# Scan stage: kernel rows of two pairs side by side in TensorE's column halves, weight transposes in two groups; attention: four probability buffers

## The chip, the core and the metric

The kernel runs on one NeuronCore of a Trainium2 chip. The metric is device time of one execution in microseconds (us). Engines are named as in the profile: PE is TensorE (PEld its weight loads), DVE is VectorE, ACT is ScalarE, POOL is GpSimd, SP is the engine that issues the DMAs here. All data is float32; the profile shows a float32 matmul as two records, one behind the other, and a transpose as one.

## The reference, cut to what matters

The reference is a first block (an S5 state-space mixer and an HGRN2 mixer, then a gated feed-forward part) and a second block of two layers, the second of which has attention with 8 heads. Two places matter here.

The S5 mixer has 64 groups of 16 channels with 64 complex states each, over 1040 tokens (padded to 1056):

```python
v_re = jnp.einsum('blgh,gph->blgp', uf, bb_re)
v_im = jnp.einsum('blgh,gph->blgp', uf, bb_im)
_, _, s_re, s_im = lax.associative_scan(_complex_affine_combine, (a_re, a_im, v_re, v_im), axis=1)
y = (jnp.einsum('blgp,ghp->blgh', s_re, c_re)
     - jnp.einsum('blgp,ghp->blgh', s_im, c_im)
     + d_skip.reshape(SSM_GROUPS, SSM_GROUP) * uf)
```

The attention of the second block takes 1024 queries against 1280 keys in 8 heads:

```python
s = jnp.einsum('bqhd,bkhd->bhqk', qi, k) * scale
p = jax.nn.softmax(s, axis=-1)
return jnp.einsum('bhqk,bkhd->bqhd', p, v)
```

## The kernel before, in words

The program is a chain of phases with a barrier of all engines between them. The change touches two: the scan (function `s5`, 937 to 1063 us of the span) and the attention (function `attend`, 2816 to 3202 us). Every engine has an instruction stream written out by hand and runs it in order; semaphores tie them together.

**Scan.** Tokens are cut in chunks of 8 (`TAU`), so that 132 chunks stand side by side (`NCH`). Two groups make a pair, whose 2 x 64 states fill the 128 partitions. There are 32 pairs, in 4 rounds (`n`) of 8; each round is worked in three trips of 3, 3 and 2 pairs, so there are 12 trips `f = 3n + trip`. The parts of the work:

- `turn(n)` on PE transposes a round's 16 input-weight tiles (4 fills of a PSUM bank with 4 transposes each); `turn_out(n)` on ACT copies each fill to `win`.
- `kernel(n)` on PE makes the kernel rows (how an input of a chunk acts on later outputs of the same chunk) of 8 pairs: for each pair four matmuls with a 128x64 weight (two parts, each with 128 and 112 columns, lines 1107 and 1108) and one with a 64x64 weight and 32 columns for the skip term (line 1110). It fills two PSUM banks, four pairs each, and uses 64 of their 128 partitions. `kernel_out(n)` on ACT copies each bank, in 8 activations, to the shifted places of `toep`.
- `inputs(f)` on PE (line 1138) brings a trip's inputs to the states, with outputs alternating between PSUM partitions 0 to 63 and 64 to 127. `turned_back(f)` and `states_of(f)` on DVE make the states of all chunks.
- `outputs(f)` on PE sums, in `psy`, `toep` times the inputs (line 1153) and the state part (line 1161). `gelus(f)` on ACT empties it (line 1223), and SP stores the result.

The order on PE for a trip f is: for trip 0, `turn(n+1)`; `inputs(f+2)`; for trip 1, `kernel(n+1)`; `outputs(f)`. On ACT it is: for trip 0, `turn_out(n+1)`; for trip 1, `kernel_out(n+1)`; `gelus(f)`; for trip 2, `spread_b(n+2)` and `decays(n+2)`. `turn` and `kernel` share the two banks of `pk`: fill number e, 6 in a round, goes to bank e % 2 and first waits for fill e - 2 to be copied out (`pk_used`). `outputs(f)` waits for `gelus(f-1)` and for the states of f. `inputs(3n)` waits for the four transposed fills of its round. SP loads the next weights to transpose (`load_wt(n+2)`) once the last of the round's four fills is made.

**Attention.** 32 steps s, four to a head (j = s % 4), two blocks of 128 queries in a step. On PE a step is: scores of the two blocks (line 2559); the 20 transposes of the probabilities of the step before in five PSUM fills (line 2589), with the sums over values between them (line 2606); and, for j = 0, 1, 2, pieces of the next head's queries and keys. ACT copies two of the five fills, then makes the two exponentials of the step (line 2695); DVE takes the row maxima (line 2781), copies three fills (line 2728), and takes the reciprocals of the sums (line 2797) once both exponentials are done; POOL then scales both blocks (line 2823), for which the next step's transposes wait. The probabilities of block i = 2s + ab are in `pr[i % 3]`: the exponential of block i waits until the transposes of block i - 3 are all made, for the second block of a step those of the same step on PE.

## Time and profile before

| | us |
|---|---|
| median of 3 runs | 3392.8 (3386.49 to 3393.48) |
| the profiled execution | 3391.3 |
| its span, first to last instruction | 3389.5 |
| around the span | 1.8 |
| scan stage, 937 to 1063 | 126 |
| attention stage, 2816 to 3202 | 386 |

Over the whole span PE is busy 3138.0 us (93%), DVE 1991.5 us, ACT 940.7 us and POOL 151.0 us. A timeline row gives start, duration, engine, line, operation, what is written and read, the shapes and a count; in square brackets stands how long the engine was idle before it and what ended that. A row with a count covers so many records from its start on. Where one row of the same engine begins before the end of the one before, the distance of the starts is the rate at which the work goes.

### The profile page before, as it was taken

The numbers are of one execution on the slowest core, as the hardware profiler recorded it, in microseconds if no ns is written. First come the engines' busy times: TensorE is split into PE (matmuls) and PEld (weight loads), VectorE is DVE, ScalarE is ACT, GpSimd is POOL, SyncE is SP. The second block draws the span as 40 slices with busy tenths as digits, with TensorE's granted clock in tenths as the row PEclk, the third lists the DMA queues.
The fourth block names the chain that finished last, engine by engine and source line by source line (L and its number), as shares of the span: only waits on it lengthen the run. The fifth ranks groups of instructions, "written<-read, shape, count | busy, mean of one in ns | idle before, by whom it ended". The sixth has DMA issues, their size and how long they took to land. (4 is left out here: it accounts for less than half of the span.)

```text
span 3389.5 us, 47701 instructions
## 1 busy us (share of the span) xinstructions
PE 3138.0 (93%) x20182; PEld 2905.0 (86%) x20182; DVE 1991.5 (59%) x2836; ACT 940.7 (28%) x1315; POOL 151.0 (4%) x124
## 2 busy tenths in 40 slices
PE   7999999998887999999999999999898977888787
PEld 7999999998876999999999998999898964555565
DVE  6666777664766455663574466444545526776446
ACT  5221222222444211211111112121323323444323
POOL 0000000000000000000000000000031001222200
PEclk9999999999988999999999999999898988999898
DMA  4223333333374344113213214111121330000121
GB/s 146 87 95 96 94 102 98 108 107 136 119 119 126 110 137 143 51 47 122 75 44 100 94 44 149 51 40 46 56 69 60 135 124 0 1 1 1 73 96 69
DMA packets 101822, 285.74 MB, mean 84 GB/s; under 512 B 13540, under 2 KB 32484, under 8 KB 100328
## 3 DMA queue, kind: packets, MB, share of 16 engines
q1 hardware_dynamic: 101608, 282.69, 26.1%
q8 instruction: 159, 2.61, 0.3%
q14 instruction: 55, 0.45, 0.0%
HBM read 218.79 MB, written 63.85 MB: 83 GB/s over the span
## 5 line engine op out<-in xcount | busy, mean ns | idle before, releaser
L471 PE MATMUL mixer_in_dense<-mix_z_high,mixer_in_whigh 128*128 128x348 f32 x1312 | 431.6, 329 | 15.3 <-DVE mixer_in_wlow L565 10.4
L471 PE MATMUL mixer_in_dense<-mix_z_high,mixer_in_wlow 128*128 128x348 f32 x1312 | 427.2, 326 | 0.0
L471 PE MATMUL mixer_in_dense<-mix_z_low,mixer_in_whigh 128*128 128x348 f32 x1312 | 426.4, 325 | 0.0
L1449 PE MATMUL flow_dense<-rst_norms_operand_b_high,flow_whigh 128*128 128x342 f32 x1248 | 399.5, 320 | 0.4 <-DVE flow_wlow L1542 0.4
L1449 PE MATMUL flow_dense<-irst_norms_operand_b_low,flow_whigh 128*128 128x342 f32 x1248 | 398.6, 319 | 0.0
L1449 PE MATMUL flow_dense<-rst_norms_operand_b_high,flow_wlow 128*128 128x342 f32 x1248 | 397.7, 319 | 0.0
L2012 PE MATMUL joint_dense<-rst_norms_operand_b_high,joint_whigh 128*128 128x342 f32 (+2 forms) x1056 | 344.6, 326 | 18.3 <-DVEq L2129 10.5
L2012 PE MATMUL joint_dense<-rst_norms_operand_b_high,joint_wlow 128*128 128x342 f32 (+2 forms) x1056 | 341.4, 323 | 0.0
L2012 PE MATMUL joint_dense<-irst_norms_operand_b_low,joint_whigh 128*128 128x342 f32 (+2 forms) x1056 | 340.4, 322 | 0.0
L1449 PE MATMUL flow_dense<-first_operand_a_high,flow_whigh 128*128 128x342 f32 (+1 forms) x912 | 291.6, 320 | 17.3 <-DVEq L1563 17.3
L1449 PE MATMUL flow_dense<-first_operand_a_low,flow_whigh 128*128 128x342 f32 (+1 forms) x912 | 292.1, 320 | 0.0
L1449 PE MATMUL flow_dense<-first_operand_a_high,flow_wlow 128*128 128x342 f32 (+1 forms) x912 | 291.4, 320 | 0.0
L471 PEld LDWEIGHTS mixer_in_dense<-mix_z_high,mixer_in_whigh 128*128 128x128 f32 x1312 | 251.6, 192 | 19.6 <-issue 16.9
L471 PEld LDWEIGHTS mixer_in_dense<-mix_z_low,mixer_in_whigh 128*128 128x128 f32 x1312 | 251.1, 191 | 0.0
L471 PEld LDWEIGHTS mixer_in_dense<-mix_z_high,mixer_in_wlow 128*128 128x128 f32 x1312 | 251.0, 191 | 0.0
L1492 ACT ACTIVATE flow_whigh<-first_norms_weights 128x1024 fp32r<-128x1024 f32 (+1 forms) x92 | 95.6, 1039 | 559.9 <-PE flow_dense L1449 536.9
L1449 PEld LDWEIGHTS flow_dense<-rst_norms_operand_b_high,flow_whigh 128*128 128x128 f32 x1248 | 235.3, 189 | 1.3 <-issue 1.2
L1449 PEld LDWEIGHTS flow_dense<-rst_norms_operand_b_high,flow_wlow 128*128 128x128 f32 x1248 | 235.2, 188 | 0.1
L1449 PEld LDWEIGHTS flow_dense<-irst_norms_operand_b_low,flow_whigh 128*128 128x128 f32 x1248 | 234.6, 188 | 0.0
L2012 PEld LDWEIGHTS joint_dense<-rst_norms_operand_b_high,joint_whigh 128*128 128x128 f32 x1056 | 202.0, 191 | 23.9 <-DVEq L2129 8.4
L2012 PEld LDWEIGHTS joint_dense<-rst_norms_operand_b_high,joint_wlow 128*128 128x128 f32 x1056 | 202.6, 192 | 0.6 <-issue 0.5
L2012 PEld LDWEIGHTS joint_dense<-irst_norms_operand_b_low,joint_whigh 128*128 128x128 f32 x1056 | 203.0, 192 | 0.0
(549 smaller groups left out, 5872.3 us busy)
## 6 DMA issues: line engine op xcount, KB each, us to landing
mixer_in_wstage<-w_in SPq DMA_DIRECT2D x56, 512.0 KB, 4.9
mixer_in_mod_w<-w_mod SPq DMA_DIRECT2D x64, 384.0 KB, 3.6
first_norms_weights<-w_up SPq DMA_DIRECT2D x44, 512.0 KB, 3.4
flow_side<-h SPq DMA_DIRECT2D x24, 512.0 KB, 5.1
h<-flow_out SPq DMA_DIRECT2D x24, 512.0 KB, 3.5
first_norms_weights<-ab_w_in SPq DMA_DIRECT2D x20, 512.0 KB, 3.5
p<-mixer_in_out SPq DMA_DIRECT2D x16, 528.0 KB, 2.8
first_norms_weights<-w_down SPq DMA_DIRECT2D x16, 512.0 KB, 3.8
```

The source lines that it names most:

```text
L471: mm = pe.matmul(bank(s)[:, 0:W], a[n % 2][:, P * m:P * (m + 1)], z[x][:, m, W * b:W * (b + 1)], start=m == 0 and i == 0, stop=m == DT - 1 ...
L1449: mm = pe.matmul(o, w[n % NW][:, P * k:P * (k + 1)], x[h][:, k, where], start=k == 0 and e == 0, stop=k == kt - 1 and e == 2)
L1492: act.activation(wh[n % NW][:, 0:w], stage[n % 2][:, 0:w], ACT.Copy).then_inc(high_ready, 1)
L2012: mm = pe.matmul(pd[s % 2][:, 0:wide], a[n % 2][:, P * k:P * (k + 1)], m, start=k == 0 and e == 0, stop=k == DT - 1 and e == 2)
```

## The change

In the scan, `kernel(n)` takes pairs two at a time: the first pair's output goes to PSUM partitions 0 to 63 and the second's to 64 to 127, with the same instructions alternating between them, so that all eight pairs fill one bank. The fills of a round are 5 instead of 6, and the one kernel fill is announced once. `kernel_out(n)` waits once and copies both halves: 16 activations, as before, now of every second pair. `turn` is called in two halves, two fills ahead of `inputs(f+2)` and two behind it. In the attention, the probabilities have four buffers instead of three, so the exponential of block i waits for the transposes of block i - 4.

```diff
--- before.py
+++ after.py
@@ -1036,7 +1036,7 @@
     urow = t["u_chunks"].rearrange("m p x -> (m p) x").rearrange("(g h) (t c) -> t h g c", h=SG, t=TAU)
     yrow = t["y_chunks"].rearrange("m p x -> (m p) x").rearrange("(g h) (t c) -> t h g c", h=SG, t=TAU)
     trips = ((0, 3), (3, 6), (6, 8))
-    NT3, TURNS, FILLS, WIDE = len(trips), 4, 6, 3
+    NT3, TURNS, FILLS, WIDE = len(trips), 4, 5, 3
     LAST = NT3 * ROUNDS
     with Phase(nc, "scan") as ph:
         U = ph.sb("u", (P, G, NCH))
@@ -1095,32 +1095,34 @@
 
                 def kernel(n):
                     pe.wait_ge(spread, n + 1)
-                    for i in range(2):
-                        o4 = bank(FILLS * n + TURNS + i)
+                    o8 = bank(FILLS * n + TURNS)
+                    for u in range(4):
+                        o = [o8[SS * side:SS * side + SS, P * u:P * u + P] for side in range(2)]
+                        first = u == 0
+                        for part in range(2):
+                            w = [bb[n % 2][part][:, 2 * u + side, :] for side in range(2)]
+                            v = [ca[:, NQ * n + 2 * u + side, part, :, :].rearrange("p k h -> p (k h)") for side in range(2)]
+                            for side in range(2):
+                                pe.matmul(o[side], w[side][:, SG:5 * SG], v[side][:, 0:P], start=first and part == 0,
+                                          stop=False, skip_group_check=True)
+                            for side in range(2):
+                                pe.matmul(o[side][:, SG:P], w[side][:, 0:4 * SG], v[side][:, 0:P - SG], start=False,
+                                          stop=False, skip_group_check=True)
+                        for side in range(2):
+                            mm = pe.matmul(o[side][:, 0:2 * SG], c["ident"][0:SS, 0:SS], skip_diag[:, NQ * n + 2 * u + side, :],
+                                           start=False, stop=True, skip_group_check=True)
+                    mm.then_inc(pk_full, 1)
+
+                def turn(n, part):
+                    if part == 0:
+                        pe.wait_ge(wt_in, 16 * (n + 1))
+                    for half in range(2):
+                        o = bank(FILLS * n + 2 * part + half)
                         for u in range(4):
-                            pair = 4 * i + u
-                            pp = NQ * n + pair
-                            o = o4[0:SS, P * u:P * u + P]
-                            for part in range(2):
-                                w = bb[n % 2][part][:, pair, :]
-                                v = ca[:, pp, part, :, :].rearrange("p k h -> p (k h)")
-                                pe.matmul(o, w[:, SG:5 * SG], v[:, 0:P], start=part == 0, stop=False, skip_group_check=True)
-                                pe.matmul(o[:, SG:P], w[:, 0:4 * SG], v[:, 0:P - SG], start=False, stop=False,
-                                          skip_group_check=True)
-                            mm = pe.matmul(o[:, 0:2 * SG], c["ident"][0:SS, 0:SS], skip_diag[:, pp, :], start=False,
-                                           stop=True, skip_group_check=True)
+                            mm = pe.transpose(o[:, P * u:P * u + P],
+                                              wt[:, part, 4 * half + u, :, :].rearrange("p k h -> p (k h)"),
+                                              c["ident"][:, :])
                         mm.then_inc(pk_full, 1)
-
-                def turn(n):
-                    pe.wait_ge(wt_in, 16 * (n + 1))
-                    for part in range(2):
-                        for half in range(2):
-                            o = bank(FILLS * n + 2 * part + half)
-                            for u in range(4):
-                                mm = pe.transpose(o[:, P * u:P * u + P],
-                                                  wt[:, part, 4 * half + u, :, :].rearrange("p k h -> p (k h)"),
-                                                  c["ident"][:, :])
-                            mm.then_inc(pk_full, 1)
 
                 def inputs(f):
                     n, trip = divmod(f, NT3)
@@ -1163,16 +1165,19 @@
                                 if part == 1 and pair == hi_ - 1:
                                     mm.then_inc(y_full, 1)
 
-                turn(0)
+                turn(0, 0)
+                turn(0, 1)
                 inputs(0)
                 inputs(1)
                 kernel(0)
                 for f in range(LAST):
                     n, trip = divmod(f, NT3)
                     if trip == 0 and n + 1 < ROUNDS:
-                        turn(n + 1)
+                        turn(n + 1, 0)
                     if f + 2 < LAST:
                         inputs(f + 2)
+                    if trip == 0 and n + 1 < ROUNDS:
+                        turn(n + 1, 1)
                     if trip == 1 and n + 1 < ROUNDS:
                         kernel(n + 1)
                     outputs(f)
@@ -1193,15 +1198,16 @@
                         [P, NQ, NCH - 1]), ACT.Copy).then_inc(decayed, 1)
 
                 def kernel_out(n):
-                    for i in range(2):
-                        e = FILLS * n + TURNS + i
-                        act.wait_ge(pk_full, e + 1)
+                    e = FILLS * n + TURNS
+                    act.wait_ge(pk_full, e + 1)
+                    for side in range(2):
                         for par in range(2):
-                            src = pk[32 * par:32 * par + 32, e % 2, :].rearrange("p (a b) -> p a b", b=P)
+                            r0 = SS * side + 32 * par
+                            src = pk[r0:r0 + 32, e % 2, :].rearrange("p (a b) -> p a b", b=P)
                             for j in range(4):
-                                ins = act.activation(toep[n % 2][32 * j:32 * j + 32, par, 4 * i:4 * i + 4, 32 * j:P],
+                                ins = act.activation(toep[n % 2][32 * j:32 * j + 32, par, side::2, 32 * j:P],
                                                      src[:, :, 0:P - 32 * j], ACT.Copy)
-                        ins.then_inc(pk_used, 1)
+                    ins.then_inc(pk_used, 1)
 
                 def turn_out(n):
                     if n >= 2:
@@ -2487,7 +2493,7 @@
         qh, ql = ([ph.sb(f"{n}{j}", (P, SEQ), F32R) for j in range(2)] for n in ("query_high", "query_low"))
         kh, kl = ([ph.sb(f"{n}{j}", (P, T2), F32R) for j in range(2)] for n in ("key_high", "key_low"))
         r1, r2 = ph.sb("turned_cos", (P, HALF)), ph.sb("turned_sin", (P, HALF))
-        pr = [ph.sb(f"probs{j}", (P, T2)) for j in range(3)]
+        pr = [ph.sb(f"probs{j}", (P, T2)) for j in range(4)]
         PT = [ph.sb(f"turned_probs{j}", (P, NKT, HALF)) for j in range(2)]
         yp, ytmp = ph.sb("attended", (P, SEQ)), ph.sb("odd_keys", (P, HALF))
         dg = ph.sb("gate", (P, 4, SEQ))
@@ -2587,7 +2593,7 @@
                                 pe.wait_ge(normal, 2 * s + ab + 1)
                             c0 = P * k if ab == 0 else (CTX + P * k if k < 8 else P * (k - 8))
                             mm = pe.transpose(o[:, 256 * kk + P * ab:256 * kk + P * ab + P],
-                                              pr[(2 * s + ab) % 3][:, c0:c0 + P], c["ident"][:, :])
+                                              pr[(2 * s + ab) % 4][:, c0:c0 + P], c["ident"][:, :])
                     mm.then_inc(full, 1)
 
                 def value_sums(H, pairs):
@@ -2690,9 +2696,9 @@
                         for ab in range(2):
                             i = 2 * s + ab
                             act.wait_ge(biased, s + 1)
-                            if i >= 3:
-                                act.wait_ge(full, ring[("t", (i - 3) // 2, 4)] + 1)
-                            act.activation(pr[i % 3][:, :], pS[:, T2 * ab:T2 * (ab + 1)], ACT.Exp, scale=scale,
+                            if i >= 4:
+                                act.wait_ge(full, ring[("t", (i - 4) // 2, 4)] + 1)
+                            act.activation(pr[i % 4][:, :], pS[:, T2 * ab:T2 * (ab + 1)], ACT.Exp, scale=scale,
                                            bias=nb[:, i:i + 1], accum_out=sm[:, i:i + 1]).then_inc(exped, 1)
                     for n in made_at(s):
                         high(n)
@@ -2820,7 +2826,7 @@
                         for ab in range(2):
                             i = 2 * s + ab
                             pool.wait_ge(inverted, s + 1)
-                            pool.tensor_scalar(pr[i % 3][:, :], pr[i % 3][:, :], ri[:, i:i + 1], 1.0, ALU.mult,
+                            pool.tensor_scalar(pr[i % 4][:, :], pr[i % 4][:, :], ri[:, i:i + 1], 1.0, ALU.mult,
                                                ALU.mult).then_inc(normal, 1)
                     H, pairs = sums_at(s)
                     if 4 in pairs and (H // 2) % 2:
```

## Rows read from the trace of the kernel before

**Rows 1.** Busy time by stage: the scan stage and the attention stage

```profile
core 0: us, PE busy (x) PEld busy (x) DVE busy (x) ACT busy (x) POOL busy (x), PEclk, DMA share, GB/s
937.00:1063.00 126.00, 107.14 (x1024) 93.42 (x1024) 89.97 (x168) 54.87 (x123) 2.16 (x2) 0.88 0.59 91
...
2816.00:3202.00 386.00, 341.18 (x1654) 201.64 (x1654) 251.28 (x346) 169.19 (x271) 95.37 (x72) 0.98 0.00 1
```

**Rows 2.** Timeline of PE inside the kernel-row matmuls of scan round 1

```profile
974.22 0.38 PE L1107 MATMUL scan_turned_and_kernel<-ssm_ca,scan_b_re 128*64 128x128 f32 x2
...
974.85 0.35 PE L1108 MATMUL scan_turned_and_kernel<-ssm_ca,scan_b_im 128*64 128x112 f32 x2
...
975.13 0.30 PE L1110 MATMUL scan_turned_and_kernel<-ssm_skip_diag,all_ident 64*64 64x32 f32 x2
...
975.36 0.43 PE L1107 MATMUL scan_turned_and_kernel<-ssm_ca,scan_b_re 128*64 128x128 f32 x2
```

**Rows 3.** Timeline of PE, matmuls whose outputs alternate between the column halves

```profile
972.82 1.57 PE L1138 MATMUL scan_v<-scan_u,scan_win 128*64 128x132 f32 x24
...
2966.68 1.08 PE L2606 MATMUL attn_values_sum<-attn_turned_probs,attn_values 128*64 128x512 f32 x4
...
2967.69 0.66 PE L2589 MATMUL attn_turned<-all_ident,attn_probs 128*128 128x128 f32 x4
```

**Rows 4.** Timeline of ACT in scan round 1: Toeplitz copies and the gelu behind

```profile
979.04 3.49 ACT L1202 ACTIVATE scan_toeplitz<-scan_turned_and_kernel 32x512 f32<-32x512 f32 x8 [5.23 <-PE scan_turned_and_kernel L1110]
...
983.81 3.49 ACT L1202 ACTIVATE scan_toeplitz<-scan_turned_and_kernel 32x512 f32<-32x512 f32 x8 [1.28 <-PE scan_turned_and_kernel L1110]
...
987.33 0.89 ACT L1223 ACTIVATE scan_yv<-scan_y 128x396 f32<-128x396 f32 x2
```

**Rows 5.** Timeline of PE in the scan, where its stages begin

```profile
963.63 1.12 PE L1120 MATMUL scan_turned_and_kernel<-all_ident,scan_wt 128*128 128x128 f32 x4 [2.99 <-ACT scan_toeplitz L1202]
...
988.30 1.17 PE L1153 MATMUL scan_y<-scan_u,scan_toeplitz 128*128 128x132 f32 x8
...
994.05 1.90 PE L1120 MATMUL scan_turned_and_kernel<-all_ident,scan_wt 128*128 128x128 f32 x8 [2.46 <-ACT scan_win L1213]
...
1002.24 0.38 PE L1107 MATMUL scan_turned_and_kernel<-ssm_ca,scan_b_re 128*64 128x128 f32 x2
...
1016.33 1.17 PE L1153 MATMUL scan_y<-scan_u,scan_toeplitz 128*128 128x132 f32 x8
...
1031.61 0.38 PE L1107 MATMUL scan_turned_and_kernel<-ssm_ca,scan_b_re 128*64 128x128 f32 x2
...
1045.69 1.17 PE L1153 MATMUL scan_y<-scan_u,scan_toeplitz 128*128 128x132 f32 x8
...
1061.05 0.50 PE L1161 MATMUL scan_y<-scan_sr,ssm_ca 64*128 64x132 f32 x4 [2.53 <-DVEq L1293]
```

**Rows 6.** Granted clock of two stretches of the scan (columns as Rows 1)

```profile
994.30:997.70 3.40, 3.40 (x24) 2.87 (x22) 2.60 (x5) 1.39 (x3) 0.00 (x0) 0.52 0.49 91
...
1021.60:1028.50 6.90, 6.36 (x36) 5.69 (x36) 5.50 (x13) 2.17 (x5) 0.00 (x0) 0.51 0.16 31
```

**Rows 7.** Waits in the attention stage: waiter, releaser, us in total, times, longest

```profile
ACT attn_probs L2695 <- PE attn_turned L2589: 22.3, 14, 1.7
```

**Rows 8.** Timeline of ACT in attention: second exponentials that waited

```profile
3003.47 1.33 ACT L2695 ACTIVATE attn_probs<-attn_scores,attn_negated_max 128x1280 f32<-128x1280 f32 x1 [1.41 <-PE attn_turned L2589]
...
3012.59 1.33 ACT L2695 ACTIVATE attn_probs<-attn_scores,attn_negated_max 128x1280 f32<-128x1280 f32 x1 [1.74 <-PE attn_turned L2589]
```

**Rows 9.** Timeline of DVE and PE behind that exponential, and DVE at the end

```profile
3003.41 0.69 DVE L2728 COPY attn_turned_probs<-attn_turned 128x512 f32<-128x512 f32 x1 [0.74 <-PE attn_turned L2589]
...
3004.92 0.17 DVE L2797 RECIPROCAL attn_inverse_sum<-attn_sum 128x2 f32<-128x2 f32 x1 [0.82 <-ACT attn_probs L2695]
...
3181.34 0.17 DVE L2797 RECIPROCAL attn_inverse_sum<-attn_sum 128x2 f32<-128x2 f32 x1 [0.82 <-ACT attn_probs L2695]
...
3007.88 0.98 PE L2589 MATMUL attn_turned<-all_ident,attn_probs 128*128 128x128 f32 x7 [0.47 <-POOL attn_probs L2823]
```

## The prediction

> **What bounds the kernel now.** I read the busy time by stage first, then each engine's timeline in the two stages that change, looking only for what ends a wait of PE. In the scan, PE is busy 107.14 of 126 us and DVE 89.97; in the attention PE is busy 341.18 of 386 us and DVE 251.28 [rows 1]. So PE sets the pace in both, with gaps in which it waits for the engine that empties its banks. None of the waits of PE in rows 5 ends with a DMA. Both stages end in a barrier and what follows starts after it, so a microsecond taken off their end comes off the total.
>
> **Scan, the kernel rows.** One pair now takes 1.14 us for the first (974.22 to 975.36), 1.19 for those behind it, eight pairs 9.5 us [rows 2]. Three of its four large matmuls take 0.63 us (974.22 to 974.85), 0.21 each. The fourth starts at 974.85, and the small one only 0.28 later, at 975.13, where 0.19 would do for its 112 columns; the next pair starts 0.23 after that, for 32 columns. Around the small one the form of the weights changes (128x64, 64x64, 128x64). So the four large ones cost 2 x 0.21 + 2 x 0.19 = 0.80 us, and the small one with both changes of form the other 0.39.
>
> With the halves alternating, the nearest row is `inputs`: 24 records, which are 12 matmuls of 132 columns, take 1.40 us (972.82 to 974.22), 0.233 for two side by side [rows 3, 2]. One alone of that width would take 0.21 x 132/128 = 0.22, so two cost little more than one. In the attention two of 512 columns take 1.01 us (2966.68 to 2967.69) [rows 3]; one alone, scaled up from 0.21, would take 0.85, a factor of 1.18. Two pairs then cost 4 x 0.233 = 0.93 by the first, or 0.80 x 1.18 = 0.94 by the second, plus 0.39 and some 0.05 for the second small one: 1.37 us, and four such couples 5.5 us instead of 9.5. The changes of form are halved in number too. If columns and not the rate of records set the time it is 5.3; if the changes of form cost as much per pair as now it is 7.1. I take 5.5, because both rows show the same alternation.
>
> Here the Trainium skill speaks against the change. "TensorE: Matmul & The Clock Gate", Part 3, The mechanism, says that a weight load overlaps running matmuls only where the row group differs, and the two halves share their rows. By that rule they would follow one another and the kernel rows stay at 9.5 us. The 0.233 us for two disagrees with it; what it would give is the first rival.
>
> **Scan, what follows the kernel rows.** The saved 4.0 us don't reach the end, because of the copies. ACT's 8 copies of a bank take 3.49 us, and the first eight now run beside the second half of PE's kernel rows; behind the last record only 3.49 us remain, and then the gelu, 0.89 us [rows 4]. After the change all 16 wait for one announcement: 6.98 us behind the last record. Queued behind them on ACT is `gelus(3n+1)`, for which PE's `outputs(3n+2)` waits, and SP's stores. From the start of the kernel rows to `outputs(3n+2)` it is now 14.1 us in each of three rounds (1002.24 to 1016.33, 1031.61 to 1045.69, and 974.22 to 988.30) [rows 2, 5]. Then: 5.5 + 0.15 to wake ACT + 6.98 + 0.92 + 0.10 = 13.65. Gain 0.43 a round, 1.3 in all. PE fills 4.5 us of ACT's time with `outputs(3n+1)` and `inputs(3n+4)` and then stands 3.6 us idle, where it has no gap now.
>
> **Scan, transposes in two groups.** From `outputs(3n+2)` to the next kernel rows it takes 13.94 us (988.30 to 1002.24) and 15.28 us (1016.33 to 1031.61) [rows 5]. PE makes two fills, then waits 2.46 us for ACT, which must first do a gelu, the spreading and the decay; then come two fills and `inputs(3n+5)`. In the new order `inputs(3n+5)`, 1.05 us for 16 records at the rate above, lies in that wait: gain 1.05 a round, 2.1 for the two. Also moved is what waits for it: the second group sits behind the inputs on PE, and SP's next load of weights waits for its last fill, but that load is needed a round later, so it costs nothing.
>
> **Scan, first round.** PE's wait of 2.99 us at 963.63 [rows 5] is for the second bank of Toeplitz copies. Now kernel(0) ends at 956.0 instead of 960.0, the 16 copies at 963.15 instead of 963.6, and the second fill waits for all of them: an idle stretch of 6.6 us. But then `inputs(2)` need nothing more. By the same durations kernel(1) starts 0.5 us earlier.
>
> **Scan, the end.** The last state part waits 2.53 us for DVE (1061.05) [rows 5]. DVE's last two chains start once `inputs(10)` are through, and these stand behind the kernel rows of round 3, which end earlier by 0.5 + 2 x (0.43 + 1.05) + 4.0 = 7.5 us; `outputs(8)`, from which PE runs to the end, starts only 0.5 + 3 x 0.43 + 2.1 = 3.9 us earlier. DVE gains 3.6 us on PE, more than the wait, which goes; ACT's gelus between the outputs are next. Gain 2.6 us. Sum for the scan: 1.3 + 2.1 + 0.5 + 2.6 = 6.5 us.
>
> **The clock.** After PE's two gaps of 2.5 us the granted clock is about half, the 1.2 GHz level (0.52 and 0.51), for 3.4 and 6.9 us [rows 6]. With all of it at full clock the 13.94 and 15.28 would be 12.4, so it costs 1.5 and 2.9 us. I leave this cost as it is. The new gaps are longer (3.6 us) and the old one shorter (1.4): the clock could recover those 4.4 us, or be low once more in each round, 1.5 us x 3.
>
> **Attention.** The second exponential of a step now never waits for the transposes of its own step. It did 14 times, 22.3 us [rows 7], of two kinds [rows 8]. Behind j = 3 of a head (3003.47, wait 1.41) the exponential runs 1.4 us earlier, but DVE's copy of the fifth fill ends at 4.10, so the reciprocal moves only from 3004.92 to about 3004.15, and POOL with it; the transposes at 3007.88, which waited for POOL, come 0.78 us earlier [rows 9]. This happens behind four of the seven heads that have another behind them, once more in the last head, and at the end, where the reciprocal at 3181.34 also trails a copy by that much [rows 9]: 6 x 0.78 = 4.7 us. The other kind (3012.59, wait 1.74 [rows 8]) gains nothing, for behind it PE has the sums over values, the next head's queries and the scores to do, and no wait for POOL follows. Behind the other three heads no wait for transposes stands at all. What is late next is DVE with its copies, still in the queue ahead of the reciprocal. Bounds: 0 if DVE is late at each place, 6 if the stall ahead of the scores goes too.
>
> **The sum.** 3391.3 - 6.5 - 4.7 = 3380.1 for the profiled execution, which lies 1.5 us below the median of the runs shown; I predict 3380.
>
> **Rivals.** First, the halves follow one another (the page's rule, as a mechanism of this kernel). Kernel rows stay 9.5 us and the copies come behind all of them: 9.5 + 8.15 = 17.65 instead of 14.1 in three rounds and 3.5 us in the first, so each microsecond of kernel rows costs four. The scan is 4 x 4.0 - 6.5 = 9.5 us longer, the total 3391.3 + 9.5 - 4.7 = 3396: slower. It decides from 8.3 us of kernel rows on. For it: one serial announcement is certain. Against: rows 3. Chance 0.08.
>
> Second, the time is swallowed by copies and clock: the new gap of 3.6 us brings a low clock in every round. Scan 6.5 - 4.5 = 2 us, total 3384.6. The skill's "TensorEngine Tiling (Array Packing)", PSUM Bottleneck, has the general form of this: tiling speeds up TensorE but not the emptying of PSUM. Rows 4 agree, with 6.98 us of copies against 5.5 of matmuls. Chance 0.18.
>
> Third, the opposite: no low clock in rounds 2 and 3: 3380.1 - 4.4 = 3375.7. Chance 0.12. Fourth, the fourth buffer does nothing, because DVE takes the place of the wait: 3384.8. Chance 0.10. My forecast, 3377 to 3384, has 0.52.
>
> **How the numbers follow.** The range takes in all but the first rival, the bounds of both sums and the 7 us by which the runs shown differ: 3372 to 3390. Some 0.2% (3386.0 to 3399.6) is what a measurement of this kernel can tell from no change. Faster: the forecast and the third case, and two thirds of the second and fourth, less what scatter takes: 0.72. Same 0.24, with half of the first rival. Slower 0.04.
>
> **What would show it.** Eight pairs of kernel rows in 5.5 us and eight matmul starts alternating; one block of 16 Toeplitz copies of 7 us behind each; a PE wait of 3 to 4 us for a gelu ahead of `outputs(2)`, (5), (8), and none of 2.5 us for DVE at the end; scan stage 119.5 us. In the attention no second exponential waiting for transposes, and the waits for POOL at 3007.88 and its like gone. It is wrong if kernel rows take over 7 us, or if the waits for POOL stay.

## The result, and the profile after

The changed kernel takes 3369.7 us, the median of four runs (3367.9 to 3376.9), against 3390.0 us (3386.5 to 3393.5) before: a ratio of 0.9944, with a 95% interval of 0.9925 to 0.9964. It is faster, by 20 us; I had forecast 11 below the profiled execution. The time lies under the low end of my range, 3372. The profiled execution took 3367.9 us (span 3366.1), 23.4 us less than the 3391.3 of the profiled one of before.

The busy times by stage of the changed kernel answer to [rows 1] (same columns). The third line is the time ahead of the scan's first `inputs`, which the change doesn't touch:

```profile
932.00:1047.00 115.00, 87.02 (x1024) 76.89 (x1024) 89.91 (x168) 55.02 (x125) 2.44 (x2) 0.88 0.64 98
2804.50:3179.00 374.50, 335.27 (x1654) 199.12 (x1654) 248.39 (x344) 166.92 (x270) 95.28 (x72) 0.99 0.00 1
0.00:941.10 941.10, 878.79 (x6342) 857.11 (x6343) 625.73 (x1000) 287.53 (x445) 11.36 (x24) 0.97 0.34 110
```

PE is busy for 20 us less in the scan than in [rows 1], with the same 1024 matmul records; DVE's 90 us are unchanged, and DVE is now the busier of the two. Its waits in the scan, in us, times and longest:

```profile
DVE scan_t L1271 <- PE scan_v L1140: 20.4, 7, 17.2
```

But for the first of 17.2 us, ahead of its first chain, it waits 3.2 us in all; before it was 17.1 (34.3 us in 7 waits, the first again of 17.2).

From the marks of both traces the 23.4 us divide like this (rounding leaves 0.1):

| stretch | before | after | gain |
|---|---|---|---|
| start to first `inputs` of the scan | 945.9 | 941.1 | 4.8 |
| scan, first `inputs` to last gelu | 117.1 | 105.7 | 11.4 |
| last gelu to first matmul of the flow | 16.5 | 17.9 | -1.4 |
| flow and what follows, up to the attention's first matmul (into `attn_scores`, against `all_ones`) | 1701.7 | 1704.8 | -3.1 |
| that matmul to first transposes of probabilities | 56.8 | 53.1 | 3.7 |
| those transposes to the last sum over values | 360.0 | 352.7 | 7.3 |
| the rest | 191.5 | 190.7 | 0.8 |

The second and the sixth line belong to the change, and so does the third, against it. SP issues the eight stores of each trip one behind another, and with the new kernel PE and ACT end the last trips faster than SP gets through them. The rows are the last stores of the scan, before and then after; in `before` the last eight start as the last gelu ends, in `after` 24 follow one another:

```profile
1063.00 3.63 SPq L1085 DMA_DIRECT2D y_chunks<-scan_yv  x8
...
1039.56 12.36 SPq L1085 DMA_DIRECT2D y_chunks<-scan_yv  x24
```

The last store is issued 3.65 us behind the last gelu before and 5.10 behind it after, and from there to the first matmul of the flow it is 12.9 and 12.8 us. So 1.4 us of what PE gained at the end of the scan stay behind with SP.

The first line is the clock: from the start to the scan's first `inputs` PE's clock stood at its 1.2 GHz level for 75 us before and for 63 us after. Over all the profiles below, with identical code up to there, that time goes from 62 to 83 us and the scan's first `inputs` start between 941.1 and 951.2; the change has no part in it. The fifth line is of the same kind: it is 53 to 54 us, with 20 to 22 us of it at the low level, or 56.7 to 57.5 us, with 28 to 30, in kernels with and without the change (56.8 in `split_alone`, 52.8 in `attn_alone`). The fourth isn't the change's either: `attn_alone`, with the old scan, took 1705.0 us there, and all the other profiles took 1702.8 to 1706.5. Why that of before was shorter, with only 3 us less at the low level, is not shown.

PE's timeline in round 1 of the scan, changed kernel, inside the kernel rows (one couple of pairs, and where the next begins), and then where the stages begin; these answer to [rows 2] and [rows 5]:

```profile
970.36 0.44 PE L1106 MATMUL scan_turned_and_kernel<-ssm_ca,scan_b_re 128*64 128x128 f32 x4
970.63 0.36 PE L1109 MATMUL scan_turned_and_kernel<-ssm_ca,scan_b_re 128*64 128x112 f32 x4
970.82 0.39 PE L1106 MATMUL scan_turned_and_kernel<-ssm_ca,scan_b_im 128*64 128x128 f32 x4
971.04 0.36 PE L1109 MATMUL scan_turned_and_kernel<-ssm_ca,scan_b_im 128*64 128x112 f32 x4
971.33 0.30 PE L1112 MATMUL scan_turned_and_kernel<-ssm_skip_diag,all_ident 64*64 64x32 f32 x4
971.57 0.44 PE L1106 MATMUL scan_turned_and_kernel<-ssm_ca,scan_b_re 128*64 128x128 f32 x4
```

```profile
958.62 1.11 PE L1122 MATMUL scan_turned_and_kernel<-all_ident,scan_wt 128*128 128x128 f32 x4 [6.60 <-ACT scan_toeplitz L1208]
...
968.00 0.39 PE L1106 MATMUL scan_turned_and_kernel<-ssm_ca,scan_b_re 128*64 128x128 f32 x4
...
972.77 1.62 PE L1155 MATMUL scan_y<-scan_u,scan_toeplitz 128*128 128x132 f32 x12
...
980.87 2.13 PE L1155 MATMUL scan_y<-scan_u,scan_toeplitz 128*128 128x132 f32 x8 [3.43 <-ACT scan_yv L1229]
...
988.23 1.14 PE L1122 MATMUL scan_turned_and_kernel<-all_ident,scan_wt 128*128 128x128 f32 x8 [1.41 <-ACT scan_win L1219]
...
993.61 0.39 PE L1106 MATMUL scan_turned_and_kernel<-ssm_ca,scan_b_re 128*64 128x128 f32 x4
...
1006.49 1.17 PE L1155 MATMUL scan_y<-scan_u,scan_toeplitz 128*128 128x132 f32 x8 [3.43 <-ACT scan_yv L1229]
```

Four records (two matmuls, one in each half) start within the 0.19 to 0.27 us that two needed. A couple takes 1.21 us (970.36 to 971.57) and eight pairs 4.77 (968.00 to 972.77), where they took 9.5. Then ACT does 7 us of copies, and PE waits 3.43 us for the gelu behind them:

```profile
972.89 7.02 ACT L1208 ACTIVATE scan_toeplitz<-scan_turned_and_kernel 32x512 f32<-32x512 f32 x16 [5.30 <-PE scan_turned_and_kernel L1112]
979.93 0.89 ACT L1229 ACTIVATE scan_yv<-scan_y 128x396 f32<-128x396 f32 x2
```

In the attention the same place as in [rows 8] and [rows 9], in another head (ACT, DVE, PE), and the one place where PE still waits long for POOL, behind the last head:

```profile
2892.02 1.33 ACT L2701 ACTIVATE attn_probs<-attn_scores,attn_negated_max 128x1280 f32<-128x1280 f32 x1 [0.22 <-DVE attn_negated_max L2789]
2893.34 1.32 ACT L2701 ACTIVATE attn_probs<-attn_scores,attn_negated_max 128x1280 f32<-128x1280 f32 x1
...
2894.78 0.69 DVE L2734 COPY attn_turned_probs<-attn_turned 128x512 f32<-128x512 f32 x1 [0.74 <-PE attn_turned L2595]
2895.39 0.15 DVE L2803 RECIPROCAL attn_inverse_sum<-attn_sum 128x2 f32<-128x2 f32 x1
...
2898.07 1.24 PE L2595 MATMUL attn_turned<-all_ident,attn_probs 128*128 128x128 f32 x8
...
3161.25 0.30 PE L2595 MATMUL attn_turned<-all_ident,attn_probs 128*128 128x128 f32 x1 [2.37 <-POOL attn_probs L2829]
```

The second exponential follows the first without a wait. The reciprocal starts 0.61 us behind the start of the copy instead of 1.51 [rows 9], and the transposes at 2898.07 wait for nothing, where those at 3007.88 waited for POOL.

### The profile page after: what moved, and what is told of

It is laid out like the page before. It is cut to its first block and busy times, and to the rows that moved or that the text cites. A ratio compares the mean times of both kernels' runs of the same rounds, so it can differ in the third digit from the quotient of the medians.

```text
span 3366.1 us, 47700 instructions
## 1 busy us (share of the span) xinstructions
PE 3107.0 (92%) x20182; PEld 2881.8 (86%) x20182; DVE 1988.9 (59%) x2836; ACT 938.6 (28%) x1315; POOL 151.0 (4%) x124
## 5 line engine op out<-in xcount | busy, mean ns | idle before, releaser
L471 PE MATMUL mixer_in_dense<-mix_z_high,mixer_in_whigh 128*128 128x348 f32 x1312 | 430.4, 328 | 15.1 <-DVE mixer_in_wlow L565 10.2
```

The lines of the kernel that those rows point to most:

```text
L471: mm = pe.matmul(bank(s)[:, 0:W], a[n % 2][:, P * m:P * (m + 1)], z[x][:, m, W * b:W * (b + 1)], start=m == 0 and i == 0, stop=m == DT - 1 ...
```

## Experiments

My theory from the two traces was: the halves overlap and the copies swallow most of that; the rest of the scan's gain is the split of the transposes, the earlier end, and the clock; the fourth buffer gives 6 to 7 us. The rivals: all of the scan's gain is the halves, or all of it is the luck of the clock. All ratios are against the kernel before, beside the same runs of it, with 95% intervals. "Stage" is the scan from its first `inputs` to its last gelu in the profile: 117.1 us before, 105.7 after.

**The parts.** `scan_alone` is the changed kernel with the three old probability buffers; `attn_alone` is the kernel before with only this edit:

```diff
-        pr = [ph.sb(f"probs{j}", (P, T2)) for j in range(3)]
+        pr = [ph.sb(f"probs{j}", (P, T2)) for j in range(4)]
...
-                            if i >= 3:
-                                act.wait_ge(full, ring[("t", (i - 3) // 2, 4)] + 1)
+                            if i >= 4:
+                                act.wait_ge(full, ring[("t", (i - 4) // 2, 4)] + 1)
```

`after_again` is the changed kernel as it is.

> The changed kernel with three probability buffers again: the scan edits alone. Theory (parts add, what is left over is the clock's phase): from the first input matmul to the last gelu the scan takes 105 to 108 us instead of 117.1, the attention stays as it was, the total is 9 to 11 us below the kernel before. Rival (the fourth buffer carries most): 4 us or less below.

> The kernel before with four probability buffers: the buffer alone. Theory: one microsecond at each of the four even heads, some 0.2 at the odd ones, and about 2 in the last head: 6 to 7 us below the kernel before. By the predicted reckoning (0.78 at six places): 4.7. Rival (the 10 us that the attention stage lost in the profiled run are all the buffer's): 10.

> The changed kernel once more. Theory: 16 to 19 us below the kernel before, and the stages ahead of the scan last as long as how often the clock is low in them says, not 5 us less than before each time. Rival (something ahead of the scan is really faster): the scan's first transposes begin near 932 us again and the low stretches ahead of it are the same as before.

Measured: `scan_alone` 3381.2 us, ratio 0.9972 (0.9961 to 0.9982), stage 105.9; `attn_alone` 3383.9, 0.9984 (0.9973 to 0.9995), first transposes to last sum over values 354.8 us instead of 360.0 (a gain of 5.2, where I had 6 to 7); `after_again` 3374.4, 0.9952 (0.9940 to 0.9964), stage 106.5. The two parts add: 0.28% and 0.16% make 0.44%, beside 0.48% and 0.56% for both together. The stage of the scan is the same with three buffers and with four, and the attention gains 5.2 us with the old scan, although this profile has 3.4 us more at the low clock than that of before.

**The two edits of the scan.** `halves_alone` is `scan_alone` with all transposes ahead of the inputs, as before:

```diff
                         turn(n + 1, 0)
+                        turn(n + 1, 1)
                     if f + 2 < LAST:
                         inputs(f + 2)
-                    if trip == 0 and n + 1 < ROUNDS:
-                        turn(n + 1, 1)
```

`split_alone` is the kernel before with this one edit in the order (and `turn` cut in two for it):

```diff
                     if trip == 0 and n + 1 < ROUNDS:
-                        turn(n + 1)
+                        turn(n + 1, 0)
                     if f + 2 < LAST:
                         inputs(f + 2)
+                    if trip == 0 and n + 1 < ROUNDS:
+                        turn(n + 1, 1)
```

> The column halves alone: transposes of a round in one group ahead of the inputs, three probability buffers. Theory: eight pairs of kernel rows in 4.8 us instead of 9.5, but from their start to the outputs of trip 2 only 1.2 us less in each of three rounds, because 16 copies stand behind them; with about 1 us in the first round and 2.5 at the end 7 us below the kernel before. Rival (the split of the transposes carries the scan's gain): 3 us or less.

> The transposes in two groups alone: six fills in a round, kernel rows in one column half, three probability buffers. Theory: one microsecond in each of two rounds, 2 us below the kernel before, and kernel rows still 9.5 us. Rival (it carries the scan's gain): 7 or more.

Measured: `halves_alone` 3388.5 us, 0.9984 (0.9974 to 0.9995), stage 112.7, a gain of 4.4 us where I had expected 7; `split_alone` 3381.8, 0.9962 (0.9951 to 0.9974), stage 109.2. The second was a miss of my theory, which gave the split 2 us: it gives 7.9 us of stage and some 12 of the total, more than the halves give, and as much as both together in `scan_alone` (0.9972). The rows say why. PE in `split_alone`, around the transposes of the next round, and then its granted clock over the whole scan behind round 0 (columns as [rows 1]):

```profile
985.39 1.09 PE L1120 MATMUL scan_turned_and_kernel<-all_ident,scan_wt 128*128 128x128 f32 x8
986.41 1.12 PE L1138 MATMUL scan_v<-scan_u,scan_win 128*64 128x132 f32 x16
988.94 1.15 PE L1120 MATMUL scan_turned_and_kernel<-all_ident,scan_wt 128*128 128x128 f32 x8 [1.41 <-ACT scan_win L1216]
...
965.00:1050.00 85.00, 77.53 (x847) 68.32 (x846) 71.64 (x136) 39.91 (x90) 0.00 (x0) 1.00 0.38 77
```

The inputs moved between the two groups fill the wait, as planned: 1.41 us stay of 2.46. But behind the shorter waits the clock does not fall at all: 1.00, where the two stretches of [rows 6] were at 0.52 and 0.51. From `outputs(3n+2)` to the next kernel rows it now takes 11.13 and 11.19 us instead of 13.94 and 15.28, so 6.9 us less; the moved inputs explain 2.1 (worked out, as in the prediction), and the clock, by what is left, the other 4.8. I had left that cost as it was.

In `halves_alone` each wait of 3.45 us for the gelu is followed by 6.8 us at the low level, in all three rounds:

```profile
989.90:996.70 6.80, 5.82 (x32) 4.94 (x32) 6.11 (x10) 2.79 (x8) 0.00 (x0) 0.55 0.45 77
1017.20:1024.00 6.80, 5.70 (x32) 4.83 (x31) 5.98 (x10) 2.84 (x8) 0.00 (x0) 0.55 0.45 75
1044.50:1051.30 6.80, 6.80 (x48) 5.98 (x48) 6.45 (x12) 0.67 (x2) 0.00 (x0) 0.55 0.44 76
```

So the halves bring a wait behind which the clock is low, and the split takes such a wait away. Together they leave a part: behind the 3.43 us the changed kernel was low for 3.4, 0 and 3.4 us, `after_again` for 6.8, 3.4 and 6.8, `scan_alone` for 3.4 three times.

**Does the alternation make the overlap?** `halves_in_turn` has the same instructions and outputs, but finishes one side of a couple before the other:

```diff
-                        for part in range(2):
-                            w = [bb[n % 2][part][:, 2 * u + side, :] for side in range(2)]
...
-                            for side in range(2):
-                                pe.matmul(o[side], w[side][:, SG:5 * SG], v[side][:, 0:P], start=first and part == 0,
+                        for side in range(2):
+                            for part in range(2):
+                                w = bb[n % 2][part][:, 2 * u + side, :]
...
+                                pe.matmul(o[side], w[:, SG:5 * SG], v[:, 0:P], start=first and part == 0,
```

> The changed kernel, but inside each couple all matmuls of the first pair go ahead of all those of the second; same fill, same copies, same places. Theory (two matmuls overlap only if neighbours in the stream lie in different halves): kernel rows back to 9.5 us, each of the four rounds 4.7 us later, 15 to 19 us above the changed kernel and near the kernel before. Rival (it is the single bank or a queue that reaches further): kernel rows stay under 6 us and the total at the changed kernel's.

Measured: 3397.0 us, 1.0014 (1.0004 to 1.0025); kernel rows 9.49 us, stage 126.3. PE inside one pair:

```profile
1002.66 0.38 PE L1106 MATMUL scan_turned_and_kernel<-ssm_ca,scan_b_re 128*64 128x128 f32 x2
1002.88 0.35 PE L1108 MATMUL scan_turned_and_kernel<-ssm_ca,scan_b_re 128*64 128x112 f32 x2
1003.07 0.38 PE L1106 MATMUL scan_turned_and_kernel<-ssm_ca,scan_b_im 128*64 128x128 f32 x2
1003.29 0.35 PE L1108 MATMUL scan_turned_and_kernel<-ssm_ca,scan_b_im 128*64 128x112 f32 x2
1003.58 0.30 PE L1110 MATMUL scan_turned_and_kernel<-ssm_skip_diag,all_ident 64*64 64x32 f32 x2
1003.80 0.43 PE L1106 MATMUL scan_turned_and_kernel<-ssm_ca,scan_b_re 128*64 128x128 f32 x2
```

The distances between the starts are those of [rows 2] to a hundredth: 0.63 us to the fourth matmul, 1.14 to the next pair. Using both halves gives nothing by itself; neighbours in the stream must be in different halves. This is also my first rival, carried out: I had worked out 3396 for it, and a scan 9.5 us longer; it is 9.2 longer. The distance to the changed kernel, 21 to 24 us by the ratios, is more than the 15 to 19 expected.

**The changes of form.** `skip_terms_last` puts the eight small skip-term matmuls behind all the large ones, so that the form of the weights changes once instead of four times there and back:

```diff
+                    for u in range(4):
+                        o = [o8[SS * side:SS * side + SS, P * u:P * u + P] for side in range(2)]
                         for side in range(2):
                             mm = pe.matmul(o[side][:, 0:2 * SG], c["ident"][0:SS, 0:SS], skip_diag[:, NQ * n + 2 * u + side, :],
```

> The changed kernel with the eight small skip-term matmuls of a round put behind all large ones, so that the form of the weights changes once and not four times. Theory (a change of form costs 0.1 to 0.2 us, the small matmul little itself): kernel rows in 4.0 to 4.3 us instead of 4.8. Rival (the small ones cost 0.3 us for two by themselves): 4.8 stays. The total moves under 3 us either way.

Measured: 3371.7 us, 0.9934 (0.9921 to 0.9947), kernel rows 3.97 us, stage 103.2. PE in its last couple, and the small ones:

```profile
999.60 0.39 PE L1106 MATMUL scan_turned_and_kernel<-ssm_ca,scan_b_re 128*64 128x128 f32 x4
999.82 0.36 PE L1109 MATMUL scan_turned_and_kernel<-ssm_ca,scan_b_re 128*64 128x112 f32 x4
1000.01 0.39 PE L1106 MATMUL scan_turned_and_kernel<-ssm_ca,scan_b_im 128*64 128x128 f32 x4
1000.23 0.36 PE L1109 MATMUL scan_turned_and_kernel<-ssm_ca,scan_b_im 128*64 128x112 f32 x4
1000.52 0.66 PE L1114 MATMUL scan_turned_and_kernel<-ssm_skip_diag,all_ident 64*64 64x32 f32 x16
```

Three changes there and back fewer save 0.80 us, 0.27 each. The edit also puts the small matmuls side by side, and no run separates that from the changes of form. The large matmuls of a couple take 0.82 us (998.78 to 999.60, the couple ahead of these rows). The kernel rows now cost 0.8 us less in three rounds, and the stage is 2.5 to 3.3 us shorter than in the two profiles of the changed kernel. The total, which I expected to move by less than 3 us, is lower by 3.4 and 6.1 us by the ratios, with intervals that overlap.

**The new wait and the clock.** `gelu_between` lets ACT do the gelu, on which PE waits, between the copies of the two halves, in the two lines that follow; `gap_filled` leaves the order alone and puts throwaway work on PE ahead of `outputs(3n+2)`, 13 matmuls against the identity into the free bank; `gap_transposes` does the same with 22 transposes. Both of these add work whose results nobody reads.

```diff
-                        kernel_out(n + 1)
+                        kernel_out(n + 1, (0,))
                     gelus(f)
+                    if trip == 1 and n + 1 < ROUNDS:
+                        kernel_out(n + 1, (1,))
```

```diff
+                def filler(n):
+                    pe.wait_ge(pk_used, FILLS * n + TURNS)
+                    o = pk[:, (FILLS * n + TURNS + 1) % 2, :]
+                    for k in range(13):
+                        pe.matmul(o[:, P * (k % 4):P * (k % 4) + P], c["ident"][:, :], c["ident"][:, :], start=True,
+                                  stop=True, skip_group_check=True)
...
+                    if trip == 2 and n + 1 < ROUNDS:
+                        filler(n + 1)
                     outputs(f)
```

> The changed kernel with ACT's gelu of trip 1 put between the two halves of the Toeplitz copies. Theory: PE's wait of 3.43 us for that gelu goes in three rounds, but VectorE, which then waits only 3.2 us in the whole scan, sets the end: 1 to 3 us below the changed kernel. Rival (the copies on ACT are the bound of the round): 3 x 3.4 = 10 us below it.

> The changed kernel with 13 throwaway matmuls of 128 columns (some 2.9 us, identity by identity, into the fill bank that is free) in each of the three waits of 3.43 us for the gelu. Theory (that gap brings the low clock behind it): no low stretch between the first round and the end, scan stage 102.5 to 104 us instead of 105.7 to 106.5, although PE does 8.7 us more work; total 1 to 3 us below the changed kernel. Rival (where the clock falls is luck): low stretches at the same places, scan stage not shorter.

> The same with 22 throwaway transposes of 128 columns (some 3.0 us) in place of the matmuls. Theory (work of any kind on PE holds the clock): as with the matmuls, no low stretch there, 102.5 to 104 us. Rival (transposes don't hold the clock): low stretches as in the changed kernel, 105 to 107 us.

Measured: `gelu_between` 3371.2 us, 0.9943 (0.9931 to 0.9955), stage 102.6; `gap_filled` 3375.7, 0.9952 (0.9939 to 0.9965), stage 102.5; `gap_transposes` 3370.0, 0.9936 (0.9924 to 0.9948), stage 102.8. PE in `gap_transposes` around the fill, and its clock over the scan behind round 0:

```profile
1002.40 2.62 PE L1172 MATMUL scan_turned_and_kernel<-all_ident 128*128 128x128 f32 x22
1005.91 1.17 PE L1155 MATMUL scan_y<-scan_u,scan_toeplitz 128*128 128x132 f32 x8 [0.88 <-ACT scan_yv L1237]
...
965.10:1046.80 81.70, 71.20 (x912) 63.38 (x910) 71.26 (x135) 40.21 (x92) 0.00 (x0) 1.00 0.39 81
```

`gap_filled` and `gap_transposes` hold the full clock in the scan behind round 0. `gelu_between` holds it up to 1045.8; there a wait of 3.31 us for DVE comes, and the last 8 us of the stage are at the low level. All three take 3 to 4 us off the stage, although in two of them `outputs(3n+2)` start no earlier with respect to the kernel rows. That part of the cost of the new wait is therefore the clock, not the waiting. Transposes hold it as matmuls do. Here the Trainium skill, "TensorE: Matmul & The Clock Gate", Part 4: PE-mode transpose, says that the clock gate's full rate doesn't engage for transposes, since they don't count as PE being busy in the same way; the 1.00 of this row disagrees with it, for transposes of 128x128 float32 put in between matmuls.

The rival for `gelu_between`, 10 us below the changed kernel, is out. In the totals little of this is to be seen: the intervals of the three overlap with both of the changed kernel (0.9944 and 0.9952).

**Without the halves, and with all that helps.** `split_and_buffers` is `split_alone` with the four buffers, so the change without its halves. `gelu_and_skip` is `gelu_between` with the skip terms last.

> The kernel before with the transposes in two groups and four probability buffers, kernel rows in one column half: the change without its column halves. Theory (the split alone gives some 8 us of the scan, the halves on top of it 3, because their copies open a gap of 3.43 us that lowers the clock): scan stage 109 us, total 0 to 4 us above the changed kernel. Rival (the halves carry the change): 7 us or more above it.

> The changed kernel with the gelu of trip 1 between the two halves of the Toeplitz copies and the skip terms behind all large matmuls. Theory (VectorE, busy 95 us in its chain, now ends the scan): 101 to 103 us for the scan, no shorter than with the gelu alone (102.6) by more than 1 us, total 3 to 5 us below the changed kernel. Rival (the two gains of 3 us add): scan under 100.5 us.

Measured: `split_and_buffers` 3376.2 us, 0.9959 (0.9948 to 0.9971), stage 109.8; `gelu_and_skip` 3367.5, 0.9933 (0.9918 to 0.9948), stage 101.8. The halves are worth 3.3 to 4.1 us of the stage (109.8 against 105.7 and 106.5) and in the total can't be told from nothing. `gelu_and_skip` has the shortest stage, and here DVE is the bound, with waits of 3.13 and 2.58 us for it near the end. Behind the first of them the clock is low for the last 17 us of the stage (0.50 from 1027.28 on), so a wait for DVE brings the low clock as one for ACT does:

```profile
1026.29 0.50 PE L1165 MATMUL scan_y<-scan_sr,ssm_ca 64*128 64x132 f32 x4 [3.13 <-DVEq L1304]
...
1035.02 0.81 PE L1165 MATMUL scan_y<-scan_sr,ssm_ca 64*128 64x132 f32 x4 [2.58 <-DVEq L1304]
```

## Why the prediction was right or wrong

Each of the three edits works as forecast, but the measured time lies under the range: three sizes and the clock were wrong, and chance came on top. In the prediction's own terms: the kernel rows stood at 5.5 us and took 4.77, which is worth 2.2 us in three rounds; the clock's cost was left as it was ("I leave this cost as it is"), and the split alone gave 4.8 us of it back, of which 1.4 are left in the whole change; the first round stood at 0.5 us and gave 1.5; the buffer stood at 4.7 and gives 5.6 to 6.9. What happened in stages that the change doesn't touch did the rest.

**The halves overlap.** Right. Two large matmuls, one in each half, take 0.205 us (0.82 for the four such of a couple in `skip_terms_last`). The rule of the Trainium skill that I had weighed against it ("TensorE: Matmul & The Clock Gate", Part 3, The mechanism: a weight load overlaps running matmuls only where the row group differs) doesn't hold here. It did not hold in the kernel before either: in its kernel rows of round 1, 974.22 to 983.71, matmuls are busy for all of the 9.49 us and weight loads for 8.01 of them, nearly all over the same 128 rows. The size was off. I had 1.37 us for a couple and 5.5 for the eight pairs; it is 1.21 and 4.77. Both of my rows [rows 3] were of wider outputs, and from them I took a surcharge of 17% for alternating that these matmuls don't pay (0.82 us for two pairs against the 0.80 worked out for one). Part of it was a slip: 4 x 0.233 is for matmuls of 132 columns, and half of these have 128 and half 112; scaled to their mean of 120 columns it would have been 0.85, not 0.93. The small matmuls with their changes of form cost 0.39 for two, as one did.

**Copies behind the kernel rows.** Right: 7.02 us, and from the start of the kernel rows to `outputs(3n+2)` 12.9 us in three rounds where I had 13.65 with the 5.5; the difference is the kernel rows. PE stands 3.43 us idle (3.6 predicted). Gain 3.6 us instead of 1.3.

**Transposes in two groups.** The wait goes from 2.46 to 1.41 us, as worked out. The step of the mechanism that failed is the sentence behind it, "I leave this cost as it is". The prediction had the right price for the clock, 4.4 us, and placed it in a rival with a chance of 0.12. `split_alone` recovers all of it. In the whole change the wait of 3.43 us brings a part back. Between the two stages it now takes 12.74 and 11.19 us: the first is 1.2 less than 13.94, the inputs alone; the second is 4.1 less than 15.28, inputs and clock. But 3.4 us at the low level then lie in the last round, 1.5 us. The net gain by the clock is 1.4 us in this profile; in `after_again`, whose stage is 0.8 us longer, less.

**First round.** The wait of 6.60 us is as worked out. From the first `inputs` to kernel(1) the gain is 1.5 us and not 0.5 (28.4 us before, 26.9 after): 0.3 up to the end of that wait, though the inputs ahead of kernel(0) took 0.7 longer at the low clock, and 1.2 behind it, where the inputs between the fills cover another wait for ACT of 0.6 us.

**The end.** The wait for DVE is gone (the last output stage takes 2.27 us instead of 4.87), as worked out: 2.6 us. Of that the 1.5 us of low clock just named come off. What the forecast missed is SP: "a microsecond taken off their end comes off the total" fails for 1.4 us, by which its stores end later behind the last gelu.

Together: 3.6 + 5.3 + 1.5 + 1.0 = 11.4 us where I had 6.5. Of the 4.9 between them, 2.2 are kernel rows in three rounds, 1.4 the clock, 1.0 the first round; 0.3 is rounding and single waits. The second rival, swallowed by copies and low clock, had the right mechanism and too large a price.

**Attention.** The mechanism is right: in `after` no exponential of the stage waits for the transposes, where 22.3 us of such waits stood [rows 7], and what follows is late by DVE's copies. PE's waits for POOL:

```profile
PE attn_turned L2595 <- POOL attn_probs L2829: 4.9, 6, 2.4
```

They were 8.2 us, 11 times. The reciprocal came 0.9 us earlier with respect to its copy, not 0.78, and from reciprocal to reciprocal three of the even heads are 1.0 us shorter (44.2 to 43.1), the last one 0.9 and the first 2.0; the odd ones, where I had expected nothing, 0.2. Some 0.8 of the 7.3 us is clock: 3.4 us at the low level lengthen a head by 0.5 to 0.9 us where they fall in one. Between profiles with equal time at the low level in this stage four buffers give 5.6 to 6.9 us (10.2 us low: 360.0 and 360.1 with three, 354.4 in `after_again` and 353.1 in `halves_in_turn` with four; 17.1 us low: 361.6 and 361.8 against 355.4 and 355.7); I had 4.7. The fourth rival, that the buffer does nothing, is out: 0.9984 with 0.9995 as the upper end.

**The range.** The terms I had mis-sized make 4.9 + 0.9 to 2.2 us, some 6 or 7. That alone would have given 3373 to 3374, near the low end but in it, and `after_again` measured 3374.4. The rest is what happens in stages the change doesn't touch: 4.8 us ahead of the scan and 3.7 ahead of the transposes by the clock, less 3.1 in the flow, in this pair of profiles. That the time fell under the range, and not just above its low end, is therefore chance. I had put 7 us of scatter into the range around 3380, but cut the low side down to the third rival and a little more.

**Open.** Why the total of `split_alone` fell by 12 us with 8 us in its stage isn't settled; its profiled run is 9.0 us under that of before, which the interval of the ratio (9 to 17 us) just holds. Whether the halves move the total at all isn't settled either: 3 to 4 us of stage, and in the total 0.9959 against 0.9952 and 0.9944, 2 to 5 us with intervals that overlap. Of what they give in the stage, 1.4 us go again to SP's stores, which end 3.66 us behind the last gelu in `split_and_buffers` and 5.04 and 5.10 in the changed kernel.

## What to carry to other kernels

Price a wait of the matmul engine together with the clock that follows it: here two waits that became 2.1 us shorter together were worth 6.9 us, and an edit that makes another engine announce later can give that back. If two small matmuls are to share the array, put them in different halves and next to one another in the stream, and gather those of another form at the end. Then look at who is busiest: here the scan passed to DVE, and at its end to the engine that issues the stores, and what PE saved after that could not come off the end.

## What the runs showed of the hardware

- Column halves over the same 128 rows overlap fully if they alternate: 4.77 us for what takes 9.49 with the same matmuls in turn.
- Three changes of the form of the weights there and back (128x64 to 64x64) fewer save 0.80 us, 0.27 a time: 4.77 against 3.97 us, with the small matmuls side by side.
- PE's waits of 2.46 to 3.45 us for ACT in the scan were nearly always followed by 3.4 or 6.8 us at the low clock level: behind all three of before (2.99, 2.46 and 2.52 us), and behind 17 of the 18 waits of 3.4 us for the gelu in the six profiles that have them. In the kernels where the longest wait behind round 0 was 1.7 us, up to the last waits for DVE, the clock stayed at 1.00. Between 1.7 and 2.46 us no run has a wait for ACT there.
- 22 transposes in a wait of 3.4 us held the clock at 1.00 as well as 13 matmuls did.
- The same 940 us of program at the head of the kernel began the scan between 941.1 and 951.2 us, with 62 to 83 us at the low level. A single pair of profiles can differ by 10 us for that alone, which is half of what this change moves.
- SP issued 24 stores of the scan in 12.36 us, 0.52 us each, and where they queued up the next stage began 1.4 us later behind the last gelu.
